# Down matrices with eleven seven-product slots a pass instead of eight, and up matrices with a slot's products sorted by form

## The reference, cut to what matters

```python
# first block, w_ff1 (2048, 8192), w_ff2 (8192, 2048)
f = jnp.square(jax.nn.relu(h @ w_ff1[l])) @ w_ff2[l]
x = x + rmsnorm(f, norm_mlp_post[l])
# second block, w_up (2048, 8192), w_down (8192, 2048)
h = h + jnp.square(jax.nn.relu(m)) @ w_down[l]
return rmsnorm_2(h, final_norm)
```

## Time and profile before

| | |
|---|---|
| median of three runs | 2242.61 us (2241.43 to 2243.77) |
| the profiled execution | 2241.2 us, of which the span of the trace is 2239.4 us |
| TensorE (PE) busy | 2213.5 us, 13180 matmuls |
| VectorE (DVE) busy | 1557.4 us |
| ScalarE (ACT) busy | 1138.0 us |
| read from HBM | 398.90 MB |

### The profile page before, as it was taken

One profiled execution on the slowest core, in us unless ns is written; L12 is line 12 of the kernel. 1 busy time (PEld: TensorE's weight loads), 2 busy tenths in 40 slices (PEclk: granted clock), 3 DMA queues, 4 the chain that ended last, 5 costly groups with the idle time before them and its releaser, 6 DMA issues.

```text
span 2239.4 us, 34020 instructions
## 1 busy us (share of the span) xinstructions
PE 2213.5 (99%) x13180; PEld 1899.9 (85%) x13180; DVE 1557.4 (70%) x1980; ACT 1138.0 (51%) x1651; POOL 93.2 (4%) x66
## 2 busy tenths in 40 slices
PE   8999999999999999999999999999999999999998
PEld 7888988888888888888898988888888888888886
DVE  6878566665555588788786578847555557879877
ACT  6432565543434365555564466736434345556545
POOL 0553000000000000000000000000000000000000
PEclk9999999999999999999999999999999999999999
DMA  8364445566666656657644433355666666656653
GB/s 325 119 154 165 153 132 216 152 187 190 185 190 185 192 196 204 212 176 261 210 149 137 168 114 113 133 190 167 178 194 180 192 180 197 211 184 204 207 179 108
DMA packets 169908, 402.43 MB, mean 180 GB/s; under 512 B 15296, under 2 KB 30912, under 8 KB 165968
## 3 DMA queue, kind: packets, MB, share of 16 engines
q1 hardware_dynamic: 158496, 394.83, 55.2%
q10 hardware_dynamic: 11312, 6.22, 1.2%
HBM read 398.90 MB, written 2.13 MB: 179 GB/s over the span
## 4 chain that ended last, share of the span: by engine, by line
PE 94%; DVE 3%; ACT 1%; issue 1%; DMA 0%; SPq 0%; ACTq 0%; DVEq 0%
PE ps L780 21%; PE ps L783 11%; PE ps L817 8%; PE ps L819 8%; PE ps L818 8%; PE ps L643 5%; PE ps L651 3%; PE ps L652 3%; PE ps L653 3%; PE ps L1051 2%; PE ps L1053 2%; PE ps L1052 2%; PE ps L831 2%; PE ps L833 2%; PE ps L832 2%; PE ps L665 2%
## 5 line engine op out<-in xcount | busy, mean ns | idle before, releaser
L2466 DVE TENSOR_TENSOR w_low<-raw_weights,w_high 128x1024 fp32r<-128x1024 f32 (+1 forms) x403 | 474.2, 1215 | 426.6 <-ACT w_high L1554 422.2
L1554 ACT ACTIVATE w_high<-raw_weights 128x1024 fp32r<-128x1024 f32 (+1 forms) x378 | 377.3, 1047 | 411.9 <-PE ps L783 283.6
L780 PE MATMUL ps<-x_split,w_high 128*128 128x512 f32 x2048 | 558.6, 394 | 1.7 <-DVE x_split L2454 1.7
L780 PEld LDWEIGHTS ps<-x_split,w_high 128*128 128x128 f32 x2048 | 350.1, 188 | 48.5 <-issue 3.0
L783 PEld LDWEIGHTS ps<-x_split,w_low 128*128 128x128 f32 x2048 | 313.7, 188 | 44.3
L783 PE MATMUL ps<-x_split,w_low 128*128 128x256 f32 x2048 | 325.9, 281 | 0.0
L817 PE MATMUL ps<-w_high,x_split 128*128 128x512 f32 x768 | 299.3, 390 | 0.0
L819 PE MATMUL ps<-w_high,x_split 128*128 128x512 f32 x768 | 299.0, 389 | 0.0
L818 PE MATMUL ps<-w_low,x_split 128*128 128x512 f32 x768 | 298.8, 389 | 0.0
L2551 DVE TENSOR_TENSOR w_low<-raw_weights,w_high 128x1024 fp32r<-128x1024 f32 x192 | 226.2, 1219 | 6.0 <-ACT w_high L1654 3.0
L1654 ACT ACTIVATE w_high<-raw_weights 128x1024 fp32r<-128x1024 f32 x192 | 191.4, 1045 | 0.0
(11 more groups left out here) (372 smaller groups left out, 3443.3 us busy)
## 6 DMA issues: line engine op xcount, KB each, us to landing
raw_weights<-in_w_ff SPq DMA_DIRECT2D x128, 1024.0 KB, 5.5
raw_weights<-in_w_up SPq DMA_DIRECT2D x64, 1024.0 KB, 5.4
raw_weights<-in_w_down SPq DMA_DIRECT2D x64, 1024.0 KB, 5.6
raw_weights<-in_w_in SPq DMA_DIRECT2D x62, 1024.0 KB, 5.5
raw_weights<-in_w_out SPq DMA_DIRECT2D x32, 1024.0 KB, 4.9
raw_weights<-in_w_mem_kv SPq DMA_DIRECT2D x7, 1024.0 KB, 14.7
residual<-in_xT SPq DMA_DIRECT2D x2, 2048.0 KB, 13.7
region<-t_table ACTq DMA_DIRECT2D x1, 3072.0 KB, 17.4
```

The costliest lines, as they stand in the source:

```text
L780: nc.tensor.matmul(o, wh[:, q, w], xs[:, kt], start=(kt == 0), stop=False, skip_group_check=True)
L1554: nc.scalar.activation(split_slot(wh_t, k)[:, r], ring_slot(n)[:, r], ACT.Copy).then_inc(rounded, 1)
L2466: V.tensor_tensor(split_slot(wl_t, k)[:, r], ring_slot(n)[:, r], split_slot(wh_t, k)[:, r].bitcast(f32), ALU.subtract).then_inc(split_read ...
```

## The change

1. Down matrices: the S slots of a pass of 32 are 2, 5, 7, 10, 12, 15, 17, 20, 22, 25 and 27 (eleven, before eight). A pass now ends S 27, P 28, P 29, P 30, P 31. The hardware loops are written out.
2. Other sums are formed, signs moved so that the weights' sums are additions. VectorE makes them with 6 instructions (before 7): two of them cover two blocks each.
3. An S slot's raw part is the whole slot (four blocks, `quad_high`, `quad_low`), the sums of weights are three blocks (before, three raw blocks and four sums). `quad_high` is rounded in two halves after the sums are made. VectorE's four subtractions are 384, 2048, 512 and 1536 elements wide (before six: 384, 1536, 1024 and three of 512).
4. TensorE runs the four products with quad first and then signals `quad_used`. With it ScalarE may write quad and the first 384 columns of `sh` for the next S slot; the rest waits for `split_used` as before. TensorE waits at two places of an S slot (before at four).
5. Up matrices: in a slot all 16 wide matmuls (`high`) come first and then the 16 narrow ones (`low`), except in the first four slots of a matrix.
6. `combine` subtracts twice where it added, and the banks' order within an S slot changes. The order of the work at the end of each pass stays.

The lists of slots:

```diff
-        PLAIN, SUMMED = {0: 0, 1: 1, 3: 2, 4: 3, 6: 4, 7: 5}, {2: 0, 5: 1}
+        SUMMED = (2, 5, 7, 10, 12, 15, 17, 20, 22, 25, 27)
+        PLAIN = tuple(r for r in range(PAIRS) if r not in SUMMED)
```

TensorE, up matrices, the new functions and their calls:

```diff
+                def high(g, w, kt):
+                    for c in range(4):
+                        nc.tensor.matmul(hidden_ps(g)[:, c], w[:, P * c:P * c + P], xs[:, kt], start=(kt == 0), stop=False,
+                                         skip_group_check=True)
+
+                def low(g, w, kt):
+                    for c in range(4):
+                        last = nc.tensor.matmul(hidden_ps(g)[:, c, 0:S], w[:, P * c:P * c + P], xh[:, kt], start=False,
+                                                stop=(kt == KT - 1), skip_group_check=True)
+                    return last
...
+                            high(g, wh[:, q], kt)
+                            if first and j < 4:
+                                last = low(g, wl[:, q], kt)
+                        if not (first and j < 4):
+                            for q in range(SK):
+                                last = low(g, wl[:, q], SK * (j % 4) + q)
```

TensorE, an S slot:

```diff
+                    pe.wait_ge(sums_ready, 2 * s + 2)
+                    pe.wait_ge(split_ready, 2 * k + 1)
+                    product(7, 2, quad_high, quad_low, 3)
+                    product(0, 0, quad_high, quad_low, 1)
+                    product(5, 1, quad_high, quad_low, 0)
+                    product(6, 6, quad_high, quad_low, 2).then_inc(quad_used, 1)
+                    pe.wait_ge(split_ready, 2 * k + 2)
                     product(1, 3, th, tl, 0)
+                    product(3, 4, th, tl, 1)
+                    product(2, 5, th, tl, 2).then_inc(split_used, 1)
```

ScalarE, the wait of a P slot (c counts the P slots), and an S slot:

```diff
+                act.wait_ge(split_used, SPLIT0[name] + (slot_before(c - 2, PLAIN) + 1 if c >= 2 else c - 1))
...
+                if c:
+                    act.wait_ge(quad_used, s)
+                else:
+                    act.wait_ge(split_used, SPLIT0[name])
+                act.wait_ge(gains_loaded, 16)
+                nc.scalar.activation(sh[:, 0:384], pair_of(r, P, 384), ACT.Copy).then_inc(sums_rounded, 1)
+                act.wait_ge(slot_loaded[n % RING], 16 * (n // RING + 1))
+                act.wait_ge(sums_made, 6 * s + 6)
+                for half_ in range(2):
+                    a = slice(SLOT // 2 * half_, SLOT // 2 * (half_ + 1))
+                    nc.scalar.activation(quad_high[:, a], w[:, a], ACT.Copy).then_inc(rounded, 1)
+                if c:
+                    act.wait_ge(split_used, SPLIT0[name] + slot_before(c - 1, SUMMED) + 1)
+                nc.scalar.activation(sh[:, 384:896], scr[:, 1536:2048], ACT.Copy).then_inc(sums_rounded, 1)
+                nc.scalar.activation(th, scr[:, 0:1536], ACT.Copy).then_inc(sums_rounded, 1)
```

VectorE, the sums of an S slot and its low parts:

```diff
+                    V.tensor_tensor(s13, x[:, 0:2], x[:, 2::-2], ALU.subtract).then_inc(sums_made, 1)
+                    dve.wait_ge(slot_loaded[n % RING], 16 * (n // RING + 1))
+                    V.tensor_tensor(t13, w[:, 1:3], w[:, 0].unsqueeze(1).to_broadcast([P, 2, 512]), ALU.add).then_inc(sums_made, 1)
+                    dve.wait_ge(sums_made, 6 * s + 1)
+                    V.tensor_tensor(s2, s1, x[:, 1], ALU.subtract).then_inc(sums_made, 1)
+                    dve.wait_ge(sums_made, 6 * s + 2)
+                    V.tensor_tensor(t2, w[:, 2], t1, ALU.add).then_inc(sums_made, 1)
+                    dve.wait_ge(sums_made, 6 * s + 3)
+                    V.tensor_tensor(s4, x[:, 3], s2, ALU.add).then_inc(sums_made, 1)
+                    dve.wait_ge(sums_made, 6 * s + 4)
+                    V.tensor_tensor(w[:, 0], w[:, 3], t2, ALU.add).then_inc(sums_made, 1)
...
+                def summed(h, r):
+                    n, k, s = SLOT0[name] + PAIRS * h + r, SPLIT0[name] + PAIRS * h + r, SUMMED0[name] + summed_count(h, r)
+                    scr = scratch_of(h, r)
+                    dve.wait_ge(sums_rounded, 3 * s + 1)
+                    V.tensor_tensor(sl[:, 0:384], pair_of(r, P, 384), sh[:, 0:384].bitcast(f32), ALU.subtract).then_inc(sums_ready, 1)
+                    dve.wait_ge(rounded, 2 * k + 2)
+                    V.tensor_tensor(quad_low, ring_slot(n), quad_high.bitcast(f32), ALU.subtract).then_inc(split_ready, 1)
+                    dve.wait_ge(sums_rounded, 3 * s + 2)
                     V.tensor_tensor(sl[:, 384:896], scr[:, 1536:2048], sh[:, 384:896].bitcast(f32), ALU.subtract).then_inc(sums_ready, 1)
+                    dve.wait_ge(sums_rounded, 3 * s + 3)
+                    V.tensor_tensor(tl, scr[:, 0:1536], th.bitcast(f32), ALU.subtract).then_inc(split_ready, 1)
```

VectorE, the order of the work of a matrix:

```diff
+                for h in range(2):
+                    if h:
+                        combine(name, 1)
+                    for r in range(PAIRS):
+                        if r == 0:
+                            sums(h, SUMMED[0])
+                        elif r + 1 in SUMMED[1:]:
+                            sums(h, r + 1)
+                        if r in SUMMED:
+                            summed(h, r)
+                        else:
+                            plain(h, r)
+                        if r == 0 and h == 0:
+                            last_summed()
+                        elif r == 0:
+                            for b in range(4):
+                                keep(name, b)
+                        elif (h, r) == (0, 1):
+                            last_squared()
 
```

More of the change, by code:

```diff
@@ L455, in program, with plain_count, summed_count, slot_before @@
         WOUT_ITERS, FF2_ITERS = KT // BODY, FT // BODY
[L457 to L470 removed]
+        PAIRS = FT // 2
+        SUMMED = (2, 5, 7, 10, 12, 15, 17, 20, 22, 25, 27)
+        PLAIN = tuple(r for r in range(PAIRS) if r not in SUMMED)
+        SUMMED0, PLAIN0 = {"ff2_1": 0, "ff2_2": 2 * len(SUMMED)}, {"ff2_1": 0, "ff2_2": 2 * len(PLAIN)}
+        BANK0 = {"ff2_1": 0, "ff2_2": 6}
+        HIDDEN_OF = {"ff2_1": 0, "ff2_2": FT // 4}
+        def plain_count(h, r):
+            return len(PLAIN) * h + sum(q < r for q in PLAIN)
+        def summed_count(h, r):
+            return len(SUMMED) * h + sum(q < r for q in SUMMED)
+        def slot_before(count, slots):
+            return PAIRS * (count // len(slots)) + slots[count % len(slots)]
+        def pair_of(r, a=0, width=512):
+            return hid_f[:, 512 * r + a:512 * r + a + width]
+        def scratch_of(h, r):
+            return sums_at[1 if (h, r) == (0, SUMMED[0]) else 0]
         def ring_slot(n):
@@ L1683, in first_product @@
                 m.own()
-                m.did(nc.scalar.activation(home[:, 1, 512:1024], ps[:, 0, :], ACT.Copy), name, "first", iters)
+                m.did(nc.scalar.activation(home[:, 1, 512:1024], ps[:, 0, :], ACT.Copy), name, "first", passes)
             def down(name, pending, between=None):
-                def body(i, later=False):
-                    for j in range(BODY):
-                        (plain if j in PLAIN else summed)(name, i, j, later)
-                        if isinstance(i, int) and (i, j) == (0, 0):
-                            pending()
@@ L2612, in down @@
-                last_summed, last_squared = up_ends
-                sums(0, 2)
-                plain(0, 0)
-                last_summed()
-                plain(0, 1)
-                last_squared()
-                rest(0)
-                with dve.Fori(1, HALF_ITERS) as i:
-                    body(i)
-                combine(name, HALF_ITERS)
-                sums(HALF_ITERS, 2, True)
-                plain(HALF_ITERS, 0, True)
-                for b in range(4):
-                    keep(name, b)
@@ L3177, in _ @@
                 final_left(t)
-            combine("ff2_2", FF2_ITERS)
+            combine("ff2_2", 2)
             for t in range(TT):
```

288 lines of the change are left out of this document (106 added, 182 removed).

## The result

The changed kernel takes 2246.43 us (median of 15 runs, 2243.66 to 2249.33), the kernel before 2241.63 in the same session (2240.91 to 2243.77): ratio 1.0022, interval 1.0015 to 1.0030. That is 4.8 us or 0.22% more, just beyond the 0.2% up to which the prediction spoke of no change, with an interval that reaches to both sides of it. The forecast was 2243.4, in a range of 2236 to 2250.5. The profiled execution of the changed kernel has a span of 2244.4 us, the one before had 2239.4: 5.0 us more, and these 5.0 are what has to be found.

A forecast was written before the change was run, and what follows sets the result against it. The prediction took TensorE's matmul stream, plus the places where it stops, as the bound. Its terms, -6.6 - 4.8 + 5.3 + 2.0 + 4.9 = +0.8 us on a median of 2242.6, gave 2243.4 us, range 2236 to 2250.5.

The forecast's parts named there:

- (a): Down stages, TensorE: twelve P slots become S slots at 0.55 us each, S slot staying at 4.87 us; -6.6 us.
- (b): Up stages, TensorE: one change from narrow to wide per slot instead of four, slot 5.57 us; -4.8 us.
- The slower rival: Up slots: the order is worth nothing or wide matmuls keep 0.2325, from 5.60 us a slot; 2248.2 to 2251.8; chance 0.16.
- VectorE and ScalarE in mid-pass: Down stages between the ends: five slots leave VectorE 1.4 us of air, the closest S handover holds; cost nothing.
- Between the passes: Down matrices: late last split delays slot (1,0), TensorE stalls 2.65 us in each of two matrices; +5.3 us.
- End of ff2_1: First down matrix's end: combine starts at E + 18.4, reduce ends up 1.7 us after TensorE's end; +2.0 us.
- End of ff2_2: Second down matrix's end: first final_whole at E + 25.3, 3.5 us behind the stream's end; +4.9 us, all in the tail.
- The ends are covered: Rival at the passes' ends: VectorE early enough in both, so -11.4, 2231.2 us; chance 0.10.
- S matmuls at 0.227: Rival in S slots: matmuls start every 0.227 us, another 4.8 us less, 2238.6; chance 0.12.
- VectorE was not the bound: Judges a rival: VectorE bounds the alternating slots, five taking over 26.1 us; at 26.5, +9, 2252 us; chance 0.08.
- the likeliest case: Whole kernel: both gains given back at the ends, by itself 2239.5 to 2247 us; chance 0.54.
- slower by over 0.2%: Whole kernel: result over 0.2% (4.5 us) slower, from the slower cases and the likeliest's edge; chance 0.21.

The follow-up runs named there:

- run 3: Changed kernel with its eleven S slots at 2, 5, 8, 10, 13, 15, 18, 21, 23, 26, 29, so a pass ends S P P: 2230.43 us.
- run 8: Changed kernel's code with eight S slots a pass at the places of the kernel before (2, 5, 10, 13, 18, 21, 26, 29): 2236.43 us.
- run 2: Kernel before with only the up matrices' new order (wide matmuls first, then narrow), down matrices untouched: 2237.31 us.
- run 1: Changed kernel with the up matrices' products back in the old order, four wide then four narrow: 2250.37 us.
- run 10: Kernel of run 5 with the early release of the quad buffers undone, so ScalarE waits for all 21 matmuls: 2236.21 us.
- run 7: Changed kernel with twelve S slots a pass (2, 5, 7, 10, 12, 15, 17, 20, 22, 24, 27, 29) and the low summed activations moved 8 words: 2232.81 us.
- Run 9: Changed kernel with TensorE's idle times between passes and behind both down matrices filled by unread transposes: 2242.27 us.
- run 5: Changed kernel with the S slots of run 3 and the low part of the summed activations moved by 8 words: 2228.18 us.
- run 6: Kernel of run 5 with high and low part of the summed activations changing places, high part at word 52128: 2231.5 us, single run.
- run 11: Kernel of run 5 with 512 of the 896 low-part words of the summed activations at word 22528, 384 staying at 52128: 2225.88 us.
- run 4: Changed kernel with only the low part of the summed activations moved by 8 words, from 52120 to 52128: 2245.38 us.

## Why the prediction held, step by step

**(a) The further S slots: -6.6 predicted, right.** The spacing 4.87 held. Taking the stalls out of the comparison, runs 3 and 8 differ by 6.5 us in their down stages and 6.0 in the median.

**(b) The up order: -4.8 predicted, -4.7 in the trace** (-2.01 and -2.69), -4.4 and -3.9 in runs 2 and 1. A slot is 5.57 us, as the sum of the earlier trace rows said. The slower rival had asked for a slot of 5.60. The formula that the prediction takes from the Trainium skill (TensorE: Matmul & The Clock Gate, Back-to-back issue gap) is in that section the gap of an isolated matmul, beside about 131 ns for a sustained stream at 512 columns; the streams here have 227 to 236 ns and depend on the order, so the measurement decides.

**VectorE and ScalarE in mid-pass: cost nothing, right, but the margin was mis-sized.** No gap stands in mid-pass. The handover's slack was about 1.4 us (estimated from run 10), not 1.9, and one more close pair (run 7) uses it up. The likely reason is in the rows of run 7, not in a run of its own: the sums of the next S slot stand in VectorE's queue ahead of the P slot's split, and I had looked at the S slot's start alone.

**Between the passes: 2 x 2.65 predicted, 2 x 2.68 measured.** The chain is the predicted one. With E, the end of the last S slot, at 932.26 in the first pass, TensorE begins slot (1,0) at E + 24.4, as predicted. At the matrix's end, where the lines above show the same chain, ScalarE's last P slot starts at 1114.17 on the word of TensorE, 0.2 us behind the end of the P slot two before it; with E at 1103.10 there, the combine starts at E + 18.3 (predicted 18.4), and the first final_whole at E + 25.3 in the second matrix (predicted 25.3). Run 3 moved the last S slot by two, changed no work, and the stalls went.

**End of ff2_1: +2.0 predicted, +3.0 to the next stage's first weights.** The reduce stands 2.1 us behind TensorE's end, as predicted within 0.4; the idle time grew by 2.5 us, and 0.5 comes from the matmuls behind it, which have a mean granted clock of 0.77 (1.00 before).

**End of ff2_2: +4.9 predicted, 4.8 measured for the wait** (7.55 us from start to start, 2.73 before), **but +6.16 in all.** The term's mechanism and size were right, and a second one behind it was missing: after 7.2 us of idle time TensorE ran most of its 32 matmuls at the lower clock, 6.19 us for 3.84.

**What the sum lacked** is thus the clock: it has no term for what TensorE runs at behind an idle time. In the profile the lower clock took 1.6 us behind the stall at 2053 (seven intervals of 0.427 for 0.227 and parts of two more), 0.5 in front of mpost's rows and 2.35 at the end, of which about 1 was given back at the very end, where the output leaves sooner after the start of the last matmul (6.15 us, before 7.15). Run 9 filled the idle times and gave 4.2 back. A fourth stretch lies in the mixer part, which the change doesn't touch; before and after, in this order:

```profile
1388.00:1394.00 6.00, 6.00 (x49) 5.07 (x49) 5.90 (x10) 3.29 (x6) 1.61 (x2) 1.00 0.34 127
```

```profile
1388.00:1394.00 6.00, 6.00 (x37) 5.21 (x36) 5.90 (x10) 3.28 (x9) 0.87 (x2) 0.72 0.24 97
```

It cost 1.2 us. The traces of runs 3, 5, 6, 10 and 11 have it too, and take 404.3 us from the last down matmul to the second up stage; those of runs 2, 7 and 8 have full clock there and take 403.0. Against it stands a gain of 1.2 us within the first 35 us of the program, in this and every other kernel with the new down code (the first wide up matmul starts at 426.0 to 426.4 us, in the kernel before and run 2 at 427.3 and 427.1). So it comes with the change; what in the code makes it is open, and the prediction had put the written-out loops at nothing. Together: +0.8 predicted, +4.7 for the clock, -1.2 at the start, and +0.7 from terms a little off make the 5.0. The forecast of 2243.4 came within 3.0 us of the median partly by luck: the gain at the start hid some of the missing term, and the kernel before, timed beside it, took 1.0 us less than the 2242.6 that the sum started from.

**The rivals.** "The ends are covered" would have given 2231.2, and run 3, whose ends are covered, takes 2230.4: the case was a matter of where the last S slots stand. S matmuls at 0.227 did not come by themselves; run 11 made most of them so. VectorE was not the bound with these eleven. The result lies on the border between the likeliest case and the prediction's "slower by over 0.2%" (0.21), and what pushed it there, the clock, is none of its rivals.

## What to carry to other kernels

Where buffers alternate between two places, the work that must be done before a stage's end is timed by the slot two before the last one. Count from the last slot of another kind, not by VectorE's share of busy time: with equal work, the order of the slots alone was worth 16 us here. Add to a predicted stall of TensorE what follows it: the matmuls behind it may run at the lower clock. And move the operands of the longest stream once, to see whether its spacing depends on where they lie.

## What the runs showed of the hardware

**The granted clock behind idle time differs from execution to execution.** Behind the same 2.52 us of idle time TensorE kept its clock at 956.70 and fell to 1.2 GHz for eight matmuls soon after 2053.49. In run 1, with the same down code, it fell behind the first stall (seven intervals of 0.427 us from 959.35 on) and not behind the second; in run 4 behind neither. In the mixer part it fell at 1389 us behind 1.0 us of idle time and some small matmuls, and in the kernel before, behind the same, it didn't. The last 48 matmuls of run 3 and of run 5 stand behind 2.3 us of idle time, in code that differs by the moved operand alone; their windows (idle, then the matmuls), run 3 first:

```profile
2213.40:2215.80 2.40, 0.14 (x1) 0.00 (x1) 2.01 (x6) 1.45 (x6) 0.00 (x0) 1.00 0.00 0
2215.80:2223.20 7.40, 7.21 (x48) 6.97 (x48) 4.94 (x13) 4.30 (x14) 0.00 (x0) 0.77 0.34 98
```

```profile
2211.70:2214.20 2.50, 0.19 (x2) 0.04 (x1) 2.11 (x6) 1.55 (x7) 0.00 (x0) 1.00 0.00 0
2214.20:2220.00 5.80, 5.55 (x48) 5.31 (x48) 4.86 (x13) 3.76 (x13) 0.00 (x0) 1.00 0.32 93
```

The spread of the changed kernel follows it: its 15 runs go from 2243.66 us at a mean clock of 0.997 to 2249.33 at 0.993, and with the idle times filled all lie within 1.4 us. The Trainium skill (TensorE: Matmul & The Clock Gate, Why this matters for your kernels) warns of idle gaps between bursts of matmuls, of longer ones than these of 1.0 to 2.5 us. By that rule the 7.2 us in front of the changed kernel's last matmuls should cost clock, and they did, 6.19 us for 3.84; behind the shorter ones the clock fell too in some executions, and there the measurement decides.

**A matmul's spacing depends on where its left operand lies.** With 14, 7 and 3 of an S slot's 21 left operands at word 52128 the slot took 4.907, 4.853 and 4.800 us. In runs 5 and 11 a product of three matmuls with one operand there is 13 ns longer than the 680 of one with none, and the other products and the P slots between keep 0.2267 a matmul. Shifting the whole operand from 52120 to 52128 gave another 0.019 a slot. What is special about the place, which lies near the end of the used memory, no run here shows.
